# Up and query products of a fused two-block kernel: one 128-column stationary tile against four 32-column strips

## What is computed

```python
h = x @ w_in[l]                        # latent and sparse attention follow
x = layer_norm(ALPHA * x + mix, ...)
q = x @ xa_wq[l]                       # cross queries: 1024 x 1024
xa = softmax(q k^T) v @ xa_wo[l]       # k, v from a 256-token memory
x = layer_norm(ALPHA * x + xa, ...)
u = x @ ffn_w_up[l]                    # conv network's up projection: 1024 x 5632
u = causal_conv3(u) + conv_b           # each channel by itself
a, g = split(u); f = (a * silu(g)) @ ffn_w_down[l]
x = layer_norm(ALPHA * x + f, ...)
```

## Time and profile before

| | |
|---|---|
| median of 3 runs | 1710.39 us |
| the profiled execution | 1710.03 us |
| its span, first to last instruction | 1708.1 us |
| mean granted TensorE clock | 0.998 of full |
| TensorE matmul busy | 1677.6 us, 98% |
| weight loads busy | 1286.7 us, 75% |
| VectorE busy | 1227.1 us, 72% |
| matmul records | 8714 |

### The profile page before, as it was taken

The page is one execution under the profiler, slowest core; times in us unless marked ns, Lnnn a source line. Parts: engine busy times, 40 slices in busy tenths (PEclk is TensorE's granted clock), DMA queues, the critical chain, the costliest instruction groups (busy, mean ns, idle before and its releaser), DMA issues.

```text
span 1708.1 us, 22812 instructions
## 1 busy us (share of the span) xinstructions
PE 1677.6 (98%) x8714; PEld 1286.7 (75%) x8714; DVE 1227.1 (72%) x2231; ACT 357.8 (21%) x902; POOL 208.2 (12%) x134
## 2 busy tenths in 40 slices
PE   8999999999999999999999999999999999999997
PEld 6887478887747887477785969994687767699953
DVE  6776376976877877483477588997844685789995
ACT  2111000024521111112271212221012531222210
POOL 1221211121020212211001000002120000000020
PEclk9999999999999999999999999999999999999999
DMA  9744455433175544445613535544447206265440
GB/s 327 234 156 148 145 182 190 133 134 124 74 231 175 191 152 176 145 144 160 222 51 118 166 123 177 170 156 165 150 125 252 98 2 222 69 228 173 154 167 25
DMA packets 163370, 266.18 MB, mean 156 GB/s; under 512 B 4104, under 2 KB 106292, under 8 KB 163134
## 3 DMA queue, kind: packets, MB, share of 16 engines
q1 hardware_dynamic: 157902, 248.72, 43.4%
q0 software_dynamic: 4624, 14.95, 2.6%
q10 hardware_dynamic: 736, 1.05, 0.3%
HBM read 262.58 MB, written 1.08 MB: 154 GB/s over the span
## 4 chain that ended last, share of the span: by engine, by line
PE 90%; DVE 5%; DVEq 2%; issue 1%; ACT 1%; DMA 1%; SPq 0%; ACTq 0%
PE psum L1014 19%; PE psum L881 15%; PE psum L1062 13%; PE psum L949 11%; PE psum L839 7%; PE psum L1272 3%; PE psum L1478 3%; PE psum L1535 3%; PE psum L1113 3%; PE psum L1186 3%; PE psum L1220 3%; PE psum L820 2%; PE psum L1101 2%; PE psum L1202 1%; DVE work L2007 1%
## 5 line engine op out<-in xcount | busy, mean ns | idle before, releaser
L699 POOL TENSOR_TENSOR work<-ring,work 128x1024 f32<-128x1024 f32 (+2 forms) x59 | 147.4, 2498 | 797.0 <-DVE work L2150 797.0
L2142 DVE TENSOR_TENSOR work<-ring 128x1024 f32<-128x1024 f32 (+2 forms) x102 | 122.0, 1196 | 83.6 <-PE psum L1062 74.3
L1062 PE MATMUL psum<-ring,work 128*128 128x512 f32 x352 | 160.9, 592 | 0.0
L2146 DVE TENSOR_TENSOR ring<-ring 128x1024 f32<-128x1024 f32 (+2 forms) x104 | 131.7, 1267 | 7.7
L2150 DVE TENSOR_TENSOR work<-ring 128x1024 f32<-128x1024 f32 (+2 forms) x102 | 122.6, 1202 | 7.6
L1062 PEld LDWEIGHTS psum<-ring,work 128*128 128x128 f32 x352 | 66.3, 190 | 81.1 <-issue 79.9
L1062 PE MATMUL psum<-work 128*128 128x512 f32 x264 | 122.5, 592 | 0.0
L1014 PE MATMUL psum<-work,ring 128*128 128x128 f32 x832 | 101.4, 275 | 0.0
L1014 PE MATMUL psum<-x_t,work 128*128 128x128 f32 x832 | 101.4, 275 | 0.0
L1014 PE MATMUL psum<-x_t,ring 128*128 128x128 f32 x832 | 97.4, 275 | 1.6 <-ACT x_t L1607 1.6
L1014 PEld LDWEIGHTS psum<-x_t,work 128*128 128x128 f32 x832 | 97.1, 192 | 0.0
(11 more groups left out here) (285 smaller groups left out, 2914.4 us busy)
## 6 DMA issues: line engine op xcount, KB each, us to landing
ring<-in_ffn_w_up_dram SPq DMA_DIRECT2D x66, 1024.0 KB, 8.0
ring<-in_w_in_dram SPq DMA_DIRECT2D x21, 2048.0 KB, 8.0
ring<-in_ffn_w_down_dram SPq DMA_DIRECT2D x20, 2048.0 KB, 7.9
ring<-in_ffn_w_gate_dram SPq DMA_DIRECT2D x22, 1024.0 KB, 5.8
ring<-in_xa_wkv_dram SPq DMA_DIRECT2D x8, 2048.0 KB, 8.5
ring<-in_w_out_dram SPq DMA_DIRECT2D x6, 2048.0 KB, 10.4
ring<-in_xa_wq_dram SPq DMA_DIRECT2D x4, 2048.0 KB, 7.9
ring<-in_xa_wo_dram SPq DMA_DIRECT2D x4, 2048.0 KB, 11.3
```

Of the source, the lines that this page charges most:

```text
L699: nc.gpsimd.tensor_tensor(t4, quarters(n, chunks, pitch)[2], t2, ALU.subtract).then_inc(fourth_ready, 1)
L1062: last = mm(sums[p], acts[p][:, q, :], rhs[:, i, :], start=(q == 0), stop=(q == KF // 2 - 1))
L2142: v.tensor_tensor(t3, b22, b12, ALU.subtract)
L2146: v.tensor_tensor(b12, b12, b11, ALU.subtract)
```

## The change

In `product` of `expand_turned` each `mm` becomes four, one for each strip of 32 output features. Operands, sums and the order of the strips' parts are as before; nothing else is edited.

```diff
-                            last = mm(corners(j)[p][:, c * P:(c + 1) * P], weights[:, i, c * P:(c + 1) * P], acts[p][:, i, :],
-                                      start=(i == 0), stop=(i == KD // 2 - 1))
+                            for r in range(0, P, 32):
+                                last = mm(corners(j)[p][r:r + 32, c * P:(c + 1) * P], weights[:, i, c * P + r:c * P + r + 32], acts[p][:, i, :],
+                                          start=(i == 0), stop=(i == KD // 2 - 1))
```

## The result

Four runs of the changed kernel took 1803.91 us (median; 1798.48 to 1806.72), the kernel before on the same chip 1710.51 us (1709.89 to 1710.68, 4 runs): a ratio of 1.0544, 95% interval 1.0531 to 1.0557. The forecast of 1710.0 us was wrong, and so was its range. The profiled execution took 1806.07 us, with a span of 1804.3, 96 us more than before.

A forecast was written before the change was run, and what follows sets the result against it. The conv networks were taken as bound by VectorE as much as TensorE from panel 0's end to `contract`'s product 3. 2 x (-0.22 - 0.02) = -0.5 us gave 1709.5, 1709.9 at the median, stated as 1710.0; range 1704.9 to 1716.

The forecast's parts named there:

- Rate: On the edited line: four strips take 0.1091 us, 0.0025 less than one full record, so 2912 records save 7.3 us.
- code-loading rival: On the edited line: 91 instruction packets, partly 0.7 us late behind ring-load bursts; +27 us, about 1738 us; chance 0.13.
- Theory C: Set up after the measurement, not in the prediction: the clock's fall is a loss of its own; no size given.
- The clock while TensorE stands: At `contract`: the clock falls while TensorE stands; priced at a few us, inside the upper range; no chance of its own.
- Changes of form: Where full matmuls and strips alternate: about 0.12 us to enter the strips' form and 0.2 us to leave it.
- Panels 1 to 10: the gain is given back at product 3: Conv networks: TensorE gains 2.8 us, then loses it waiting for VectorE at product 3 of `contract`; net zero.
- the prediction's sum of -0.5 us: Whole kernel, two layers: -0.22 us up to panel 0's end and -0.02 us in the queries, each doubled.
- VectorE bound: Conv networks from panel 0's end: VectorE is saturated, about 12.9 us a panel against TensorE's 12.5.
- The faster rival: Conv networks: VectorE moves with TensorE and is not the bound, so 5.5 us come off, 1704.9 us; chance 0.06.
- Lost pace: On the edited line: strips issued at half the pace, 0.218 us a round, +310 us, 2020 us and more; chance 0.05.

## Why the prediction was wrong, and where it was right

**The step that failed** is *Rate*, in its bound from above: that the pace of L1490, seen for 64 records, lasts. The pace of a round was right: between two packets that come in time lie 32 rounds in 3.49 us, 0.109 each. But the line's time was taken as rounds times pace, 7.3 us less, and the code's supply was left to a rival, at a chance of 0.13. One packet holds 3.5 us of such work, and the code comes every 3.3 to 4.3 us on a quiet DMA and every 7.6 at worst beside bursts. What the runs showed in the term's place is 93.9 us more in the four stretches: 70 us in which TensorE stood and 24 us more of busy time (353.2 against 328.9), which fits the 47.8 us at half clock.

**The code-loading rival was what happened, and its price was wrong.** It gave +27 us, and it was +93. Packets of 256 instructions, one held ahead, bursts that block: all as it said. Mis-sized was how late a packet comes. It took half of a burst plus 0.9 us and "0.7 us too late" on half of the 91 packets: 32 us. The stalls over 0.7 us number 29 and last 2.6 us each on average, 75.5 in sum. Two terms were missing. On an idle queue a packet starts 1.1 us after the border and can be used 2.2 to 3.2 after that, so it is on time by nothing even without a burst, and then each part of a burst that it meets counts in full. And the clock: the trace has 13 stretches at 1.2 GHz, 47.8 us in all, against 0 in these stages before; half of that at most, 24 us, is lost. Without the burst, the same packets cost 17 us (1727.4 against 1710.1); from there to 1743.5 with some bursts and 1803.9 with all. Theory C is only partly apart: the clock's fall goes with the length of the stalls (13 stretches where the listed idle times are 1.98 us on average, 3, 1 and none where they are 1.05, 0.84 and 0.49). Stalls without the clock's fall there were, 17 us with nearly no loads and, but for 3.4 us at most, 61 us with paced loads; a kernel at the low clock without stalls there was not, so the 24 us rest on the records of the clock and of busy time alone.

The prediction held against the rival that "nothing shows that only one packet is held". Nothing showed more than one either: in the profile before, a packet of this line lasted 14 us, two bursts. The Trainium skill's sentence "Only 2 cache lines!" ("Advanced Engine Details and Errata", ISA Cache) was the better half of the two that the prediction quoted; the packet that starts after a border is the one missed at the next border, as two lines of 256 instructions give; eight lines, an estimate of 28 us of such work from the page's 128 KB, would have ridden through any burst seen here.

**The clock while TensorE stands** was priced at a few us, at `contract`. It fell elsewhere, inside the stage.

**Changes of form** fit as far as two strips of 64 can show it: the conv network's line is 2.86 us shorter in each layer, where rate and entries gave 3.0, and the queries' line 0.27 us. For strips of 32 the stalls cover them.

**Panels 1 to 10: the gain is given back at product 3** could not be seen in the changed kernel, since it had no gain left. With strips of 64 it came as forecast: no stall of code, 1709.55 us against a forecast of 1710.0, the wait for L2729 in both layers. That the total agrees with the prediction's sum of -0.5 us is partly luck: the kernel before beside it took 1709.99 us, and the interval of the ratio, 0.9988 to 1.0007, holds no change as well.

**VectorE bound.** Shown from both sides: slowed, it takes both forms to the same 1725 us; with its one wait removed (by two edits together, whose shares no run separates), the strips' gain comes through as 3.4 us. The faster rival (TensorE's whole 5.5 us count) falls. Of the 5.7 us by which the conv networks' line got shorter, 3.4 arrive; the other 2.3 were followed only to ScalarE's copy L1933 (L1935 there), for which TensorE stands 1.6 us before `contract` in the two layers; the rest stays open.

**Lost pace** (2020 us) falls: a round takes 0.109 us across whole packets, 27 ns a record, where the rival had 0.218 us a round or 62 ns a matmul.

## What to carry to other kernels

Before an operation is split, compare the time of 256 of the engine's instructions (weight loads count too) with the time in which the code queue brings as many: here about 4 us on a quiet DMA, and from a border up to 5.1 + 2.5 = 7.6 us beside bursts of loads. Splitting in two left 7 us a packet and cost nothing (its latest packet started 3.2 us after the border), splitting in four left 3.5 and cost 5%. And where two engines are tied, a gain on one shows only once the single wait at which it is given back has been found and moved: look at the last semaphore of the stage, and at what it really has to protect.

## What the runs showed of the hardware that was not expected

- With strips of 32, an instruction packet starts most often 1.1 us after TensorE has crossed into the packet before it, and beside bursts 3.1 to 5.1 us; where the engine stood, it goes on 1.2 to 1.6 us after the transfer has ended, once 1.9.
- Cutting loads into pieces of 512 KB keeps the clock (0.997) and makes the stalls shorter, but more of them: 56 for 35.
- The granted clock falls to 1.2 GHz among the stalls, and 60 records then take 3.29 us for 1.91 (the window around them has a granted clock of 0.55).
- A sum of 1024 columns on GpSimd holds one of VectorE's taps for 2.1 us.
- A weight load's wait of 0.56 us in front of a matmul cost nothing.
